# Output projection of an attention block: the two column halves of a token tile multiplied in one run of 48 products, the weights split in that order

## The chip, the cores and the metric

The kernel runs on one core of a Trainium2 chip. The metric is the device time of one execution in microseconds (us), the median of several runs. The engines are PE (TensorE: matmul products and transposes; PEld are its weight loads), ACT (ScalarE), DVE (VectorE), POOL (GpSimd) and SP (SyncE, which only issues DMAs here).

## The reference

One layer of a hybrid encoder block on x of 2048 tokens by 1024 columns, in float32:

```python
h = rms_norm(x, norm_mix_pre[l])
proj = h @ w_in[l]
...
mixed = jnp.concatenate([out_a, out_b], axis=-1) @ w_out[l]
x = x + rms_norm(mixed, norm_mix_post[l])
h = rms_norm(x, norm_ffn_pre[l])
f = (jax.nn.silu(h @ w_gate[l]) * (h @ w_up[l])) @ w_down[l]
x = x + rms_norm(f, norm_ffn_post[l])
```

`out_a` (512 columns) comes from sliding-window attention, `out_b` (512 columns) from differential attention. The change touches the third line alone, the product with `w_out` (1024 by 1024), and what surrounds it.

## The kernel before

The program is four stages, one after the other, with a barrier of all engines between them (`m.end()`): `proj_phase` (norm, projection, sliding-window attention), `diff_attn`, `out_proj` and `ffn`. Every engine has its own written-out program and they meet on semaphores, so the order of the work on each engine is the order of the code.

`out_proj` (line 1357) goes over 16 tiles of 128 tokens. It multiplies in float32 precision by splitting each operand into a high part (`_hi`) and the rest (`_lo`); one product becomes three, hi x hi, hi x lo, lo x hi (line 1662). For a tile k the steps are:

- SP loads the sliding-window part already transposed (`swa_in`) and the differential part by rows (`mix_in`), lines 1427 and 1428.
- PE transposes `mix_in` (`turn_m`, four transposes, line 1648). ACT makes `mt_hi` of both parts (`hi_m`, lines 1537 and 1539), POOL and DVE make `mt_lo` (`split_swa`, line 1485; `lo_m`, line 1592).
- PE multiplies: `multiply(n, k, i)` does column half n, 8 contraction chunks c by 3 products of 512 columns = 24 products into one PSUM bank. The stationary operand is the tile (`mt_hi` or `mt_lo`, chunk c), the moving one the weights.
- ACT sums the squares of y (`square_y`, line 1548), POOL makes the factor of the norm (`y_rstd_of`), DVE applies it (`norm_y`, line 1602), POOL adds x (`add_x`, line 1506).
- ACT sums the squares of the new x (`square_x`, line 1556), POOL makes the second factor (`x_rstd_of`, lines 160 and 162), DVE applies it and writes `h_row` (`norm_x`, line 1610).
- PE transposes `h_row` (`turn_h`, eight transposes, line 1674), ACT and DVE split the result (`hi_h`, `lo_h`, lines 1564 and 1617), SP stores it for the feed-forward stage.

The engines are staggered by one tile. In its pass k PE does `multiply(0, k)`, `turn_m(k+1)`, `multiply(1, k)`, `turn_h(k-1)`. In the same pass the others do, in this order:

```python
# ACT, lines 1575 to 1582
square_y(k - 1, i)
hi_m(k + 1, i)
square_x(k - 1, i)
hi_h(k - 1, i)
# DVE, lines 1630 to 1637
norm_y(k - 1, i)
lo_m(k + 1, i)
norm_x(k - 1, i)
lo_h(k - 1, i)
```

`hi_m(k+1)` waits in its middle, at line 1538, for `m_turned`, which `turn_m(k+1)` raises. y uses PSUM banks 0 to 3, so each tile has two of its own and the next tile the other two; the transposes use banks 4 to 6 in turn.

The weights come in 16 pieces of 128 by 512 (line 1373). Eight buffers hold them raw, ACT makes `w_hi` (line 1573), DVE `w_lo` (line 1627), each piece in turn. PE in tile 0 waits for each piece (line 1661).

Of the kernel before, what the change touches and what calls it, by code (L numbers as in the profile page):

```python
# [33 lines left out]
KC = D // P  # L34
# [21 lines left out]
def steady(count, k, i):  # L56

    return count(k) if i is None else (count(k + 2) - count(k)) * i + (4 * count(k) - 3 * count(k + 2))


def tiles(eng, first=0, end=TILES):


    for k in range(first, 6):
        yield k, None
    with eng.Fori(3, TILES // 2 - 1) as i:
        yield 6, i
        yield 7, i
    for k in range(TILES - 2, end):
        yield k, None  # L70
# [1286 lines left out]
def out_proj(nc, x, swa_t, mixed, w_out, subln, g_post, g_ffn, x_mid, h_s, h_hl):  # L1357
# [10 lines left out]
    y_banks, t_banks = Banks([0, 1, 2, 3], y_order), Banks([4, 5, 6], t_order)  # L1368
    SC = QA // P
    HW = D // 2  # L1370

    RAW = 8
    pieces = [(c, slice(n * HW, (n + 1) * HW)) for n in range(2) for c in range(KC)]

    with ExitStack() as ctx:
        m = Memory(nc, ctx, "op")
        ps = m.psum()
# [25 lines left out]
        w_hi_done, w_lo_done = m.sem("w_hi_done"), m.sem("w_lo_done")  # L1403
# [3 lines left out]
        m_turned, swa_hi, swa_lo, m_hi, m_lo = (m.sem(n) for n in ("m_turned", "swa_hi", "swa_lo", "m_hi", "m_lo"))  # L1407
        multiplied, y_squared, y_normed, pool_step, y_rstd_ready = (
            m.sem(n) for n in ("multiplied", "y_squared", "y_normed", "pool_step", "y_rstd_ready"))
# [6 lines left out]
        read_out = {"y": (y_normed, lambda t, n: 2 * t + n + 1), "m": (m_lo, lambda t: t + 1),  # L1416
                    "h": (h_lo, lambda t, n: 2 * t + n + 1)}

        with nc.Block() as block:
# [222 lines left out]
            @block.tensor  # L1642
            def _(pe):
                def turn_m(k, i):
                    pe.wait_ge(in_loaded[k % 2], steady(lambda t: 32 * (t // 2 + 1), k, i))
                    t_banks.free(pe, read_out, k, i, "m")
                    for j in range(DW // P):
                        last = pe.transpose(ps[:, t_banks.bank("m", k), j * P:(j + 1) * P],
                                            mix_in[:, k % 2, j * P:(j + 1) * P], ident[:, :])
                    last.then_inc(m_turned, 1)  # L1650

                def multiply(n, k, i):
                    q = k % 2
                    if n == 0:
                        pe.wait_ge(swa_lo, steady(lambda t: t + 1, k, i))
                    y_banks.free(pe, read_out, k, i, "y", n)
                    for c in range(KC):
                        if n == 0 and c == SC:
                            pe.wait_ge(m_lo, steady(lambda t: t + 1, k, i))
                        if k == 0:  # L1660
                            pe.wait_ge(w_lo_done, n * KC + c + 1)
                        for j, (lhs, rhs) in enumerate(((mt_hi, w_hi), (mt_hi, w_lo), (mt_lo, w_hi))):
                            last = pe.matmul(ps[:, y_banks.bank("y", k, n), :], lhs[:, q, c, :],
                                             rhs[:, c, n * HW:(n + 1) * HW],
                                             start=(c == 0 and j == 0), stop=(c == KC - 1 and j == 2))
                    last.then_inc(multiplied, 1)

                def turn_h(k, i):
                    pe.wait_ge(h_ready, steady(lambda t: t + 1, k, i))
                    for n in range(2):  # L1670
                        t_banks.free(pe, read_out, k, i, "h", n)
                        for j in range(4):
                            at = (4 * n + j) * P
                            last = pe.transpose(ps[:, t_banks.bank("h", k, n), j * P:(j + 1) * P], h_row[:, at:at + P],
                                                ident[:, :])
                        last.then_inc(h_turned, 1)

                pe.wait_ge(consts_made, 2)
                turn_m(0, None)
                for k, i in tiles(pe):  # L1680
                    multiply(0, k, i)
                    if k + 1 < TILES:
                        turn_m(k + 1, i)
                    multiply(1, k, i)
                    if k >= 1:
                        turn_h(k - 1, i)
                turn_h(TILES - 1, None)
# [316 lines left out]
def hybrid_block(nc, x, w_in, sinks, lambda_q1, lambda_k1, lambda_q2, lambda_k2, subln, w_out, g_mix_pre, g_mix_post,  # L2004
                 g_ffn_pre, g_ffn_post, w_gate, w_up, w_down, rope, out):

    def scratch(name, shape):
        return nc.dram_tensor(name, shape, F32, kind="Internal").ap()

    swa_t = scratch("swa_t", (P, QA // P, S))  # L2010
    q_s = scratch("q_s", (TILES, P, DH, 2, P))
    k_s = scratch("k_s", (P, DH, 2, S))
    v_s = scratch("v_s", (P, DH, TILES, VD))
    mixed = scratch("mixed", (S, DW))
    x_mid = scratch("x_mid", (S, D))
    h_s = scratch("h_s", (P, KC, 2, S))
    proj_phase(nc, x, w_in, g_mix_pre, sinks, rope, swa_t, q_s, k_s, v_s)
    diff_attn(nc, q_s, k_s, v_s, [lambda_q1, lambda_k1, lambda_q2, lambda_k2], mixed)
    with nc.sbuf_tensor("h_hl", [P, KC, 2, TB], F32R) as h_hl:
        out_proj(nc, x, swa_t, mixed, w_out, subln, g_mix_post, g_ffn_pre, x_mid, h_s, h_hl)  # L2020
        ffn(nc, h_s, h_hl, x_mid, w_gate, w_up, w_down, g_ffn_post, out)
# [40 lines left out]
```

## Time and profile before

| what | us |
|---|---|
| three runs: lowest, median, highest | 2763.47, 2764.42, 2766.68 |
| span of the profiled execution, first to last instruction | 2758.1 |
| PE busy in the span | 2567.2 (93%) |
| weight loads (PEld) busy | 2129.6 (77%) |
| DVE, ACT, POOL busy | 1265.5, 1082.0, 680.5 |

The profiled execution has only its span: the median of the runs lies 6.3 us above it, which is what surrounds the first and the last instruction and how one execution differs from another. `out_proj` takes from about 1057 us to 1283 us of the span. PE is busy almost all of the time, but that is an average over stages, and a stage has to be read by itself. "Granted clock" or PEclk is the clock that PE was given, as a share of 2.4 GHz: 1.0 is 2.4 GHz, 0.5 is 1.2 GHz. A timeline row gives the start, the length, the engine, the line, the operation with what it writes <- reads, and in brackets how long the engine sat idle before it and what ended that. Neighbouring rows of one kind are merged (x4).

### The profile page before, as it was taken

What the parts mean: (1) busy time and instruction counts of PE and PEld (TensorE: products, weight loads), DVE (VectorE), ACT (ScalarE), POOL (GpSimd) and SP (SyncE); (2) the same over time, 40 slices, a digit from 0 to 9 for tenths busy, and PEclk for the clock granted to TensorE, in tenths of its full rate; (3) what the DMA queues carried; (4) which work ended last, traced back from release to release, by engine and by line L of the source; (5) the groups of instructions that cost most, each with busy time, mean ns of one, the idle gap of its engine ahead of it and who ended that gap; (6) DMA issues with size and microseconds to landing.
All of it is one profiled execution on the core that took longest, in us unless ns stands there. A gap on an engine that the chain in (4) does not pass through costs nothing.

```text
span 2758.1 us, 38624 instructions
## 1 busy us (share of the span) xinstructions
PE 2567.2 (93%) x12588; PEld 2129.6 (77%) x12588; DVE 1265.5 (46%) x2315; ACT 1082.0 (39%) x2326; POOL 680.5 (25%) x827
## 2 busy tenths in 40 slices
PE   7999989996887887996999999999999999999997
PEld 5888867875776776885888888888888888888886
DVE  5667775556887884333222224222242222332223
ACT  5555563334666664332444223332222222233221
POOL 1323222223756654341111003110021110111101
PEclk9999989998999998998999999999999999999999
DMA  5111123334323214766333425334253343433332
GB/s 168 41 52 52 52 69 120 129 115 137 95 65 88 81 38 162 234 215 219 94 96 99 155 82 170 96 99 157 72 178 96 99 155 96 136 115 99 98 93 84
DMA packets 190193, 310.52 MB, mean 113 GB/s; under 512 B 15600, under 2 KB 119024, under 8 KB 190064
## 3 DMA queue, kind: packets, MB, share of 16 engines
q1 hardware_dynamic: 186608, 296.42, 34.3%
q0 software_dynamic: 3456, 12.58, 1.4%
q8 instruction: 56, 0.92, 0.1%
q14 instruction: 73, 0.60, 0.1%
HBM read 246.03 MB, written 62.91 MB: 112 GB/s over the span
## 4 chain that ended last, share of the span: by engine, by line
PE 52%; DVE 0%; issue 0%; DMA 0%; ACT 0%; POOL 0%; ACTq 0%; DVEq 0%; POOLq 0%
PE ff_psum L1963 35%; PE ff_psum L1993 17%; DVE ff_y L1917 0%; DMA ff_w_raw<-in_w_gate_dram 0%; DVE ff_y L1949 0%; DVE ff_y L1909 0%; ACT ff_junk L1861 0%; DVE ff_w_lo L1895 0%; ACT ff_w_hi L1888 0%; POOL ff_rstd L162 0%; ACTq L1741 0%; POOL ff_rstd L1819 0%; POOL ff_rstd L160 0%; ACTq L1844 0%; ACTq L1751 0%
## 5 line engine op out<-in xcount | busy, mean ns | idle before, releaser
L1963 PE MATMUL ff_psum<-h_hl,ff_w_hi 128*128 128x512 f32 x2816 | 869.4, 390 | 18.6 <-DVE ff_w_lo L1895 14.0
L1895 DVE TENSOR_TENSOR ff_w_lo<-ff_w_raw,ff_w_hi 128x1024 fp32r<-128x1024 f32 x264 | 328.5, 1246 | 986.0 <-ACT ff_w_hi L1845 974.4
L1963 PEld LDWEIGHTS ff_psum<-h_hl,ff_w_hi 128*128 128x128 f32 x2816 | 529.5, 188 | 130.1 <-DVE ff_w_lo L1895 14.4
L1845 ACT ACTIVATE ff_w_hi<-ff_w_raw 128x1024 fp32r<-128x1024 f32 x263 | 278.1, 1060 | 843.0 <-PE ff_psum L1963 500.0
L1963 PE MATMUL ff_psum<-h_hl,ff_w_lo 128*128 128x512 f32 x1408 | 548.7, 390 | 0.0
L1963 PEld LDWEIGHTS ff_psum<-h_hl,ff_w_lo 128*128 128x128 f32 x1408 | 265.0, 188 | 55.4
L1810 POOL TENSOR_TENSOR ff_g_lo<-ff_gated,ff_g_hi 128x512 f32 x88 | 113.4, 1290 | 759.5 <-ACT ff_g_hi L1852 759.2
L1993 PE MATMUL ff_psum<-ff_w_hi,ff_g_hi 128*128 128x512 f32 x704 | 273.9, 389 | 0.0
L1993 PE MATMUL ff_psum<-ff_w_lo,ff_g_hi 128*128 128x512 f32 x704 | 273.9, 389 | 0.0
L1993 PE MATMUL ff_psum<-ff_w_hi,ff_g_lo 128*128 128x512 f32 x704 | 273.9, 389 | 0.0
L1218 ACT ACTIVATE da_probs<-da_psum,da_bias 128x512 f32<-128x512 f32 (+3 forms) x320 | 196.1, 622 | 73.0 <-DVE da_bias L1270 60.8
L1264 DVE TENSOR_REDUCE da_tops<-da_psum 128x1 f32<-128x512 f32 (+3 forms) x288 | 173.8, 620 | 26.9 <-PE da_psum L1325 22.5
L1348 PE MATMUL da_psum<-da_values,da_at 128*128 (+1 forms) x1088 | 150.1, 281 | 19.1 <-ACT da_at L1226 11.0
L1348 PEld LDWEIGHTS da_psum<-da_values,da_at 128*128 128x128 f32 x1088 | 139.2, 194 | 34.6 <-issue 19.5
L1325 PE MATMUL da_psum<-da_keys,da_q_hl 128*128 (+3 forms) x320 | 139.4, 438 | 28.4 <-DMA da_keys<-k_s 16.8
L1993 PEld LDWEIGHTS ff_psum<-ff_w_lo,ff_g_hi 128*128 128x128 f32 x704 | 132.1, 188 | 27.6
L1993 PEld LDWEIGHTS ff_psum<-ff_w_hi,ff_g_lo 128*128 128x128 f32 x704 | 132.1, 188 | 27.4
L1993 PEld LDWEIGHTS ff_psum<-ff_w_hi,ff_g_hi 128*128 128x128 f32 x704 | 132.1, 188 | 27.3
L1325 PE MATMUL da_psum<-da_keys,da_q_lh 128*128 (+3 forms) x320 | 119.8, 377 | 0.0
L1184 POOL TENSOR_TENSOR da_probs<-da_probs 128x512 f32<-128x512 f32 (+2 forms) x96 | 116.7, 1216 | 8.0
L1852 ACT ACTIVATE ff_g_hi<-ff_gated 128x512 f32 (+1 forms) x88 | 55.6, 632 | 150.4 <-issue 150.4
L1819 POOL TENSOR_TENSOR ff_rstd<-ff_ss 128x4 f32<-128x4 f32 x4 | 0.8, 202 | 461.1 <-ACT ff_junk L1861 461.1
(192 smaller groups left out, 4215.4 us busy)
## 6 DMA issues: line engine op xcount, KB each, us to landing
ff_w_raw<-in_w_gate_dram SPq DMA_DIRECT2D x88, 512.0 KB, 3.6
ff_w_raw<-in_w_up_dram SPq DMA_DIRECT2D x88, 512.0 KB, 3.6
ff_w_raw<-in_w_down_dram SPq DMA_DIRECT2D x88, 512.0 KB, 3.6
pp_x<-in_x_dram SPq DMA_DIRECT2D x32, 512.0 KB, 4.7
h_s<-op_ht SPq DMA_DIRECT2D x16, 1024.0 KB, 6.2
h_hl<-h_s SPq DMA_DIRECT2D x3, 4096.0 KB, 14.4
pp_w_raw<-in_w_in_dram SPq DMA_DIRECT2D x32, 256.0 KB, 4.6
k_s<-pp_dk_hl SPq DMA_DIRECT2D x16, 512.0 KB, 4.0
```

What stands on the lines that cost most here:

```text
L1184: pool.tensor_tensor(probs[:, q, 0, cols], probs[:, q, 1, cols], probs[:, q, 0, cols], ALU.add)\
L1218: act.activation(probs[:, q, m, 4 * P * c:4 * P * c + w], ps[:, b, 0:w], ACT.Exp, bias=bias[:, r, m:m + 1], accum_out=sums[:, r, m, c:c + ...
L1264: top = dve.tensor_reduce(tops[:, r, m, c:c + 1], ps[:, b, 0:w], AX.X, ALU.max)
L1325: last = pe.matmul(ps[:, b, 0:w], stack[:, s % Q_SLOTS, m, :], keys[:, bass.ds(h, 1), m, 4 * P * c:4 * P * c + w].squeeze(1), start=(j == ...
L1348: last = pe.matmul(ps[:, O_BANK, 0:VD], at[:, n % A_SLOTS, j, :], values[:, bass.ds(h, 1), 4 * c + j, :].squeeze(1), start=(c == 0 and j = ...
L1810: pool.tensor_tensor(g_lo[:, bass.ds(f, 1), :].squeeze(1), gated[:, q, :], g_hi[:, bass.ds(f, 1), :].squeeze(1).bitcast(F32), ALU.subtract ...
L1819: pool.tensor_tensor(rstd[:, :], ss[:, 0, :], ss[:, 1, :], ALU.add).then_inc(pool_step, 1)
L1845: act.activation(w_hi[:, slot, :], w_raw[:, slot, :], ACT.Copy).then_inc(w_hi_done, 1)
L1852: act.activation(g_hi[:, bass.ds(f, 1), :].squeeze(1), gated[:, q, :], ACT.Copy).then_inc(g_hi_done, 1)
L1895: dve.tensor_tensor(w_lo[:, slot, :], w_raw[:, slot, :], w_hi[:, slot, :].bitcast(F32), ALU.subtract)\
L1963: last = pe.matmul(ps[:, u, :], w[:, u, at], h_hl[:, c, a, :], start=(c == 0 and n == 0), stop=(c == KC - 1 and n == 2))
L1993: last = pe.matmul(ps[:, bank, :], g[:, f, j * P:(j + 1) * P], w[:, u % R, rhs], start=(f == 0 and i == 0), stop=(f == FC - 1 and i == 2))
```

## The change

`multiply` takes both halves of a tile: for each chunk c and each of the three products it multiplies half 0 and then half 1 with the same stationary operand, 48 products in a row. Since there is only one run, `turn_m(k + 1)` stands behind all 48 instead of between the halves. The pieces of the weights are listed by chunk, then by half, and tile 0 waits for two pieces per chunk. Both banks have to be free, and `swa_lo` is waited for, before the first product; `m_lo` is waited for at chunk 4, which is now product 25 of 48. Nothing of ACT, DVE, POOL or SP is edited but the order of the 16 pieces.

```diff
@@ -1370,7 +1370,7 @@
     HW = D // 2
 
     RAW = 8
-    pieces = [(c, slice(n * HW, (n + 1) * HW)) for n in range(2) for c in range(KC)]
+    pieces = [(c, slice(n * HW, (n + 1) * HW)) for c in range(KC) for n in range(2)]
 
     with ExitStack() as ctx:
         m = Memory(nc, ctx, "op")
@@ -1649,21 +1649,23 @@
                                             mix_in[:, k % 2, j * P:(j + 1) * P], ident[:, :])
                     last.then_inc(m_turned, 1)
 
-                def multiply(n, k, i):
+                def multiply(k, i):
                     q = k % 2
-                    if n == 0:
-                        pe.wait_ge(swa_lo, steady(lambda t: t + 1, k, i))
-                    y_banks.free(pe, read_out, k, i, "y", n)
+                    pe.wait_ge(swa_lo, steady(lambda t: t + 1, k, i))
+                    for n in range(2):
+                        y_banks.free(pe, read_out, k, i, "y", n)
                     for c in range(KC):
-                        if n == 0 and c == SC:
+                        if c == SC:
                             pe.wait_ge(m_lo, steady(lambda t: t + 1, k, i))
                         if k == 0:
-                            pe.wait_ge(w_lo_done, n * KC + c + 1)
+                            pe.wait_ge(w_lo_done, 2 * c + 2)
                         for j, (lhs, rhs) in enumerate(((mt_hi, w_hi), (mt_hi, w_lo), (mt_lo, w_hi))):
-                            last = pe.matmul(ps[:, y_banks.bank("y", k, n), :], lhs[:, q, c, :],
-                                             rhs[:, c, n * HW:(n + 1) * HW],
-                                             start=(c == 0 and j == 0), stop=(c == KC - 1 and j == 2))
-                    last.then_inc(multiplied, 1)
+                            for n in range(2):
+                                last = pe.matmul(ps[:, y_banks.bank("y", k, n), :], lhs[:, q, c, :],
+                                                 rhs[:, c, n * HW:(n + 1) * HW],
+                                                 start=(c == 0 and j == 0), stop=(c == KC - 1 and j == 2))
+                                if c == KC - 1 and j == 2:
+                                    last.then_inc(multiplied, 1)
 
                 def turn_h(k, i):
                     pe.wait_ge(h_ready, steady(lambda t: t + 1, k, i))
@@ -1678,10 +1680,9 @@
                 pe.wait_ge(consts_made, 2)
                 turn_m(0, None)
                 for k, i in tiles(pe):
-                    multiply(0, k, i)
+                    multiply(k, i)
                     if k + 1 < TILES:
                         turn_m(k + 1, i)
-                    multiply(1, k, i)
                     if k >= 1:
                         turn_h(k - 1, i)
                 turn_h(TILES - 1, None)
```

PE in a pass before, from the last three products of half 0 to the first of the next tile (`op_mt` is the tile, `op_w` the weights, `op_mix_in` the rows that `turn_m` turns, `op_h_row` those of `turn_h`):

```order
L1663 MATMUL op_psum<-op_w_hi,op_mt_hi 128x512
L1663 MATMUL op_psum<-op_w_lo,op_mt_hi 128x512
L1663 MATMUL op_psum<-op_w_hi,op_mt_lo 128x512
L1648 MATMUL op_psum<-op_ident,op_mix_in 128x128 x4
L1663 MATMUL op_psum<-op_w_hi,op_mt_hi 128x512
...
L1663 MATMUL op_psum<-op_w_hi,op_mt_lo 128x512
L1674 MATMUL op_psum<-op_ident,op_h_row 128x128 x8
L1663 MATMUL op_psum<-op_w_hi,op_mt_hi 128x512
```

24 products stand between the two sets of transposes. PE at the same place now:

```order
L1664 MATMUL op_psum<-op_w_hi,op_mt_hi 128x512 x2
L1664 MATMUL op_psum<-op_w_lo,op_mt_hi 128x512 x2
L1664 MATMUL op_psum<-op_w_hi,op_mt_lo 128x512 x2
L1648 MATMUL op_psum<-op_ident,op_mix_in 128x128 x4
L1676 MATMUL op_psum<-op_ident,op_h_row 128x128 x8
L1664 MATMUL op_psum<-op_w_hi,op_mt_hi 128x512 x2
```

No product stands between them any more; they follow each other in this way in the passes k = 1 to 14. ACT in one pass, before and now alike (`op_y_junk` is `square_y`, `op_mt_hi` is `hi_m`, `op_x_junk` is `square_x`, `op_ht` is `hi_h`):

```order
L1548 ACTIVATE op_y_junk,op_y_ss<-op_psum 128x512 x2
L1537 ACTIVATE op_mt_hi<-op_swa_in 128x512
L1539 ACTIVATE op_mt_hi<-op_psum 128x512
L1556 ACTIVATE op_x_junk,op_x_ss<-op_x_new 128x1024
L1564 ACTIVATE op_ht<-op_psum 128x4x128 x2
```

On ACT nothing moved: the operation that needs the turned `op_mix_in` (L1539) stands ahead of the one that leads to `op_h_row` (L1556).

## Rows read from the trace of the kernel before

**Rows 1.** Busy time in a stretch of out_proj: length, then each engine, PEclk, DMA share, GB/s

```profile
core 0: us, PE busy (x) PEld busy (x) DVE busy (x) ACT busy (x) POOL busy (x), PEclk, DMA share, GB/s
...
1200.00:1260.00 60.00, 60.00 (x290) 49.08 (x289) 21.98 (x28) 22.05 (x49) 25.70 (x35) 1.00 0.61 198
```

**Rows 2.** Timeline, out_proj, one tile: start us, length us, engine, line, operation

```profile
1099.55 0.60 PE L1648 MATMUL op_psum<-op_ident,op_mix_in 128*128 128x128 f32 x4
...
1100.18 0.60 ACT L1539 ACTIVATE op_mt_hi<-op_psum 128x512 fp32r<-128x512 f32 x1 [3.72 <-PE op_psum L1648]
...
1101.21 1.06 ACT L1556 ACTIVATE op_x_junk<-op_x_new 128x1024 bf16<-128x1024 f32 x1 [0.43 <-POOL op_x_new L1506]
...
1103.38 1.29 DVE L1610 SCALAR_TENSOR_TENSOR op_h_row<-op_x_new,op_x_rstd,op_ffn_row 128x1024 f32<-128x1024 f32 x1 [1.88 <-POOL op_x_rstd L162]
...
1105.58 1.04 PE L1674 MATMUL op_psum<-op_ident,op_h_row 128*128 128x128 f32 x8
...
1112.06 0.60 PE L1648 MATMUL op_psum<-op_ident,op_mix_in 128*128 128x128 f32 x4
```

**Rows 3.** Timeline of PE, out_proj: the 24 products behind op_mix_in: first, second, last

```profile
1099.90 0.48 PE L1663 MATMUL op_psum<-op_w_hi,op_mt_hi 128*128 128x512 f32 x1
1100.22 0.39 PE L1663 MATMUL op_psum<-op_w_lo,op_mt_hi 128*128 128x512 f32 x1
...
1105.35 0.40 PE L1663 MATMUL op_psum<-op_w_hi,op_mt_lo 128*128 128x512 f32 x1
```

**Rows 4.** Page, costliest groups: products and weight loads of one stationary operand used twice

```profile
L1963 PE MATMUL ff_psum<-h_hl,ff_w_hi 128*128 128x512 f32 x2816 | 869.4, 390 | 18.6 <-DVE ff_w_lo L1895 14.0
...
L1963 PEld LDWEIGHTS ff_psum<-h_hl,ff_w_hi 128*128 128x128 f32 x2816 | 529.5, 188 | 130.1 <-DVE ff_w_lo L1895 14.4
```

**Rows 5.** Timeline of PE, feed-forward stage, up part (L1963)

```profile
1499.75 0.62 PE L1963 MATMUL ff_psum<-h_hl,ff_w_hi 128*128 128x512 f32 x2
```

**Rows 6.** Timeline of PE, feed-forward stage, down part (L1993): 12 products in a row

```profile
1599.71 0.39 PE L1993 MATMUL ff_psum<-ff_w_hi,ff_g_hi 128*128 128x512 f32 x1
...
1602.20 0.39 PE L1993 MATMUL ff_psum<-ff_w_hi,ff_g_lo 128*128 128x512 f32 x1
```

**Rows 7.** Timeline, end of out_proj: PE waits for h_row

```profile
1278.21 1.28 DVE L1610 SCALAR_TENSOR_TENSOR op_h_row<-op_x_new,op_x_rstd,op_ffn_row 128x1024 f32<-128x1024 f32 x1 [4.69 <-POOL op_x_rstd L162]
...
1279.55 1.97 PE L1674 MATMUL op_psum<-op_ident,op_h_row 128*128 128x128 f32 x8 [10.57 <-DVE op_h_row L1610]
```

**Rows 8.** Timeline of PE: idle times of earlier stages, with their releasers

```profile
370.76 0.66 PE L844 MATMUL pp_psum<-pp_ident,pp_probs 128*128 128x128 f32 x2 [4.18 <-DVE pp_o_sum L715]
...
691.87 0.33 PE L1336 MATMUL da_psum<-da_ident,da_probs 128*128 128x128 f32 x1 [2.38 <-POOL da_probs L1184]
...
837.68 0.58 PE L1348 MATMUL da_psum<-da_values,da_at 128*128 x1 [4.24 <-DVE da_at L1297]
...
943.00 0.72 PE L1348 MATMUL da_psum<-da_values,da_at 128*128 x2 [3.17 <-DVE da_at L1297]
```

**Rows 9.** Stretches right behind those idle times (columns as in rows 1)

```profile
370.76:376.28 5.52, 5.52 (x19) 4.77 (x20) 3.48 (x9) 3.89 (x8) 1.20 (x3) 0.50 0.29 92
...
837.68:840.49 2.81, 2.81 (x11) 2.51 (x12) 2.21 (x11) 0.40 (x2) 1.23 (x2) 0.50 0.00 0
...
943.00:946.31 3.31, 3.31 (x14) 3.01 (x15) 2.64 (x12) 0.56 (x4) 1.64 (x3) 0.52 0.04 9
...
691.87:695.30 3.43, 3.43 (x26) 3.18 (x26) 3.42 (x6) 2.58 (x9) 3.17 (x4) 1.00 0.00 0
```

**Rows 10.** Timeline, start of out_proj: products at the low clock, last weights

```profile
1067.15 0.76 PE L1663 MATMUL op_psum<-op_w_hi,op_mt_hi 128*128 128x512 f32 x1 [4.54 <-DVE op_w_lo L1627]
...
1067.71 0.63 PE L1663 MATMUL op_psum<-op_w_lo,op_mt_hi 128*128 128x512 f32 x1
...
1068.14 0.63 PE L1663 MATMUL op_psum<-op_w_hi,op_mt_lo 128*128 128x512 f32 x1
...
1077.13 2.78 DVE L1627 SCALAR_TENSOR_TENSOR op_w_lo<-op_w_raw,op_sub_col,op_w_hi 128x512 fp32r<-128x512 f32 x4
```

## The prediction

> **What bounds the kernel now.** I read the granted clock and the busy times first, then the stretches of the stage that the change touches, then its timeline. In `out_proj` PE is busy for the whole of each steady stretch at the full clock, while DVE, ACT and POOL are each busy for less than half of it [rows 1]. So in this stage any time in which PE newly waits is added to the kernel, and work saved on another engine is worth nothing.
>
> The timeline of one tile shows what this cover rests on [rows 2]. PE begins the transposes of tile k+1's `op_mix_in` at 1099.55, goes on with 24 products, and at 1105.58 begins the transposes of tile k-1's `op_h_row`. Between these two times the others work through a chain that begins with PE's own transposes: ACT L1539 starts at 1100.18, ACT L1556 at 1101.21, then POOL's two small steps, DVE L1610 from 1103.38 for 1.29 us. `op_h_row` is ready at 1104.67, 0.91 us before PE wants it. The next tile's transposes begin at 1112.06, so a tile costs 12.51 us.
>
> **The change, part by part.**
>
> *The products.* 48 a tile before and after, none removed and none added, and each half keeps its own 24. Behind `op_mix_in`, from the start of the second of 24 products to that of the last is 5.13 us for 22 steps, 0.233 us each [rows 3]. What could change is that the second product of a pair has the same stationary operand. The feed-forward stage shows such pairs: there each product has its own weight load, 2816 for 2816 [rows 4], and two of them together take 0.62 us where one takes 0.39, so the second starts 0.23 us after the first [rows 5]. The kernel before also uses `mt_hi[c]` for two products in turn at that even pace. I take 0. For the lower bound, the twelve down products step at 2.49 / 11 = 0.226 us [rows 6]: 768 products by 0.007 us would save 5.3 us. For the upper bound, the new order changes PSUM bank at each product. The down part changes bank after every six with nothing visible in its even steps; a change of bank costs 0.01 us there at most, the last digit of the rows, so at most 768 x 0.01 = 7.7 us.
>
> The Trainium skill, "TensorE: Matmul & The Clock Gate", section "Step-by-step: what each phase is for", says that the weight load is its own instruction because a loaded operand can serve many products. The trace shows no product without its load, so it has no case of this. The same page's Part 1 gives 215.7 ns from start to start of full-clock products of 512 columns; by that figure the run would gain 768 x 17.5 ns, an estimated 13.4 us.
>
> *The transposes of `op_mix_in` move behind product 48.* They are the same four; what moves with them is the start of the chain. ACT does L1539 (`hi_m`) before L1556 (`square_x`), so tile k-1's `square_x` cannot start until tile k+1's `op_mix_in` is turned, and `turn_h(k-1)` now stands right behind those four transposes. Counting from their start, T: ACT L1539 starts at T + 0.63 and takes 0.60; L1556 follows at about T + 1.23, since `add_x` has by then ended long ago (before, L1556 waited 0.43 us for it; now it has the time of 24 products more). From the start of L1556 to that of DVE L1610 is 1103.38 - 1101.21 = 2.17 us, L1610 takes 1.29 [rows 2], and PE starts 0.06 us after its end, as at the end of the stage [rows 7]. That is T + 4.75. Without a wait PE would go on at T + 0.35, as the first product behind the transposes does (1099.90) [rows 2, 3]. The new wait is 4.40 us of PE a tile. DVE's L1592 (`lo_m`) lies beside it and ends before L1610 can start. The wait occurs where both sets of transposes stand together: k = 1 to 14, 14 times, **61.6 us**. If ACT's two operations overlap somewhat it is 4.1 us (57.4 in all); if nothing of the 0.35 counts, 4.75 (66.5).
>
> Nothing else becomes late. Behind the wait stand `turn_h` and then tile k+1; its `mt_hi` and `mt_lo` are all made within the wait, so `m_lo` at product 25 costs nothing. ACT's `hi_h(k-1)` and `square_y(k)` lie behind `turn_h` as before, and the chain from there to `add_x` fits under the 48 products, 11.2 us. SP's loads for tile k+2 and its stores follow the same semaphores and have a whole tile. In the last pass there is no `turn_m`, so `turn_h(14)` has no new wait, and the last tile's idle time of 10.57 us [rows 7] stays: in both orders ACT takes both squares of tile 15 after `hi_h(14)`.
>
> *The clock.* PE did nothing for 4.18, 4.24 and 3.17 us in three places of the earlier stages [rows 8], and right behind each the granted clock was 0.50 to 0.52, which is the level of 1.2 GHz, for 5.52, 2.81 and 3.31 us of work, a mean of 3.88. After an idle time of 2.38 us it was 1.00 [rows 9]. The new waits are like the first three. At the low level a product takes 1068.14 - 1067.71 = 0.43 us instead of 0.233 [rows 10], so 0.455 of the time is lost. 3.88 x 0.455 = 1.76 us a wait, 14 times **24.7 us**. The bounds are the shortest and the longest stretch: 1.28 and 2.51 us, 17.9 and 35.1 in all.
>
> The same page, section "HAM oscillation — how this bites in real kernels", tells of a kernel whose PE waits in each pass and starts each pass at the low clock, and prices this at half of the low time. By that the term would be 14 x 3.88 x 0.5, an estimated 27.2 us. The rows' 0.455 is what I use.
>
> *The weights by chunk.* The first product now waits for two pieces, one more than at 1067.15; a piece is 2.78 / 4 = 0.70 us of DVE [rows 10]. These 0.70 us fall at the low clock, so some 1.6 products are put off, 1.6 x 0.233 = 0.4 us. At the far end the last piece is ready at 1077.13 + 2.78 = 1079.91 [rows 10] in both orders; three products stood behind it and now six do, at most 3 x 0.233 = 0.7 us more. I take **0.4 us**, between 0 and twice a piece, 1.4.
>
> *Sum.* 61.6 + 24.7 + 0.4 = 86.7 us, on a span of 2758.1: 2844.8. The 6.3 us by which the median lies above the profiled span are not touched, so 2764.4 + 86.7 = **2851 us**.
>
> **The rivals.**
>
> *The wait comes, the clock holds.* For it: the 2.38 us row. Against it: all three rows of over 3 us. 2764.4 + 61.6 + 0.4 = 2826 us.
>
> *The clock does not come back within a tile.* Then all 48 products run at 0.43 us, 9.4 us lost a tile: 2764.4 + 62 + 14 x 9.4 = 2958 us. Against it: behind every idle time of the rows the work brought the clock back in at most 5.52 us, and a tile has 11 us or more of dense products.
>
> *The reuse pays, and the kernel is not slower.* The mechanism is the second product of each pair going without the cost of a load, its place is the 384 second products. It has to give back 86.7 us, 0.226 us for each: they would have to be nearly free. The rows of pairs in the feed-forward stage show the second one at the full 0.23 us. If all it gave were the 0.007 us a product seen between stages, the time would be 2846. By the page's 215.7 ns it would be an estimated 2838. Should the four transposes not hold up `op_h_row` after all, so that this gain stood alone, the time would be 2764.4 + 0.4 - 5.3 = 2760 us; the order of ACT speaks against that.
>
> **How the numbers follow.** Forecast, wait and clock together: 0.89. Wait without the clock: 0.05. Clock stays down: 0.02. A small gain of pace beside the waits is inside the forecast. Not slower, by the last rival: 0.03, of which faster 0.02 and same 0.01; the remaining 0.01 is some other slower case. A measurement of this kernel tells about 0.2%, 5.5 us, from no change, so faster means under 2759 and slower over 2770: 0.02, 0.01, 0.97. The lower end is 2764.4 + 57.4 + 17.9 - 5.3 = 2834. The upper ends together are 2764.4 + 66.5 + 35.1 + 1.4 + 7.7 = 2875; all four at once is less likely than one of them, and I stop at 2870.
>
> **What would show each step.** In a timeline of a steady tile: four transposes, then an idle time of PE of about 4.1 us ended by DVE's `op_h_row` (L1610), then eight transposes; 14 such waits, 57 to 60 us, in the table of waits. ACT L1556 right behind L1539. PEclk near 0.5 just behind each wait and 1.0 before the end of the tile, a tile of 18 to 19 us instead of 12.5. Products at 0.233 us where the clock is full; 768 weight loads still. The stage ends some 87 us later, the others unchanged. I am wrong if `op_h_row` is ready when PE arrives, if the waits number other than 14, if the clock stays at 1.0, or if products at the full clock step at something other than 0.23 us.

## The result and the profile after

| | us |
|---|---|
| after, median of 4 runs (lowest, highest) | 2849.07 (2846.85, 2851.14) |
| before, median of 4 runs beside it | 2763.94 |
| ratio, 95% interval | 1.0313 (1.0301 to 1.0326) |
| span of the profiled execution, before and after | 2758.1, 2847.8 |

The change makes the kernel 85 us slower, 3.1%. Of all executions behind the figures of this document one, of e1 below, was slow (3298.40 us at a granted clock of 0.74) and is left out of its ratio. The first lines of the page after:

```profile
span 2847.8 us, 38628 instructions
...
PE 2599.4 (91%) x12588; PEld 2154.9 (76%) x12588; DVE 1266.2 (44%) x2315; ACT 1081.7 (38%) x2326; POOL 682.6 (24%) x827
```

PE is busy for 32 us more than before for the same products, and the span is 89.7 us longer. Neither says where; the stretches do. Up to 1057 us PE's busy time is 922.2 us before and 923.1 after, in the feed-forward stage 1440.1 and 1440.2. In `out_proj` it is 204.9 and 236.1.

The timeline of one tile after, all engines, at the place of [rows 2] (in the changed file the transposes of `op_h_row` are line 1676, the products line 1664; ACT, DVE and POOL keep their lines here):

```profile
1169.50 0.60 PE L1648 MATMUL op_psum<-op_ident,op_mix_in 128*128 128x128 f32 x4
1170.13 0.60 ACT L1539 ACTIVATE op_mt_hi<-op_psum 128x512 fp32r<-128x512 f32 x1 [10.04 <-PE op_psum L1648]
1170.63 1.05 ACT L1556 ACTIVATE op_x_junk<-op_x_new 128x1024 bf16<-128x1024 f32 x1
1170.76 0.69 DVE L1592 TENSOR_TENSOR op_mt_lo<-op_psum,op_mt_hi 128x512 fp32r<-128x512 f32 x1 [8.48 <-ACT op_mt_hi L1539]
...
1171.91 0.19 POOL L160 TENSOR_SCALAR op_x_rstd<-op_x_ss 128x1 f32<-128x1 f32 x1 [5.83 <-issue]
...
1172.77 1.28 DVE L1610 SCALAR_TENSOR_TENSOR op_h_row<-op_x_new,op_x_rstd,op_ffn_row 128x1024 f32<-128x1024 f32 x1 [1.32 <-POOL op_x_rstd L162]
...
1174.11 1.97 PE L1676 MATMUL op_psum<-op_ident,op_h_row 128*128 128x128 f32 x8 [4.02 <-DVE op_h_row L1610]
```

The transposes of `op_mix_in` start at 1169.50. ACT takes them at +0.63 and begins `square_x` (L1556) at +1.13, POOL's first step comes at +2.41, DVE's `op_h_row` at +3.27, and PE goes on at +4.61, idle for 4.02 us by the bracket. In [rows 2] the same operations stand between the same two points, with 24 products of PE beside them.

The table of waits in the stage (engine and line <- what it waited for: us in all, times, longest):

```profile
ACT op_mt_hi L1539 <- PE op_psum L1648: 149.6, 16, 11.1
...
PE op_psum L1676 <- DVE op_h_row L1610: 67.2, 15, 10.6
```

15 waits for `op_h_row`: the one of 10.6 us at the end of the stage, that was there before [rows 7], and 14 new ones that make up 56.6 us. ACT's wait for the turned `op_mix_in` went from 49.3 to 149.6 us, which costs nothing by itself: it is the other side of the same move, since ACT now stands at L1539 for the whole run of products, and `square_x` behind it.

Stretches after, in the columns of [rows 1]: products before a wait, the first and the second part of the wait, the work right behind it, the rest of the tile, and the work behind the next wait.

```profile
1159.00:1169.40 10.40, 10.40 (x46) 8.37 (x45) 1.56 (x3) 1.10 (x3) 4.57 (x5) 0.99 0.79 252
1170.11:1172.77 2.66, 0.00 (x0) 0.00 (x0) 0.69 (x1) 1.63 (x3) 0.74 (x2) 1.00 0.00 0
1172.79:1174.11 1.32, 0.00 (x0) 0.00 (x0) 1.27 (x1) 0.00 (x0) 0.00 (x0) 0.50 0.00 0
1174.11:1179.61 5.50, 5.50 (x17) 4.73 (x18) 1.64 (x3) 2.87 (x7) 0.94 (x3) 0.50 0.13 43
1179.62:1187.50 7.88, 7.88 (x35) 6.34 (x35) 1.14 (x2) 0.00 (x0) 3.64 (x2) 1.00 0.97 316
1193.49:1196.67 3.18, 3.18 (x12) 2.89 (x13) 1.24 (x2) 1.77 (x5) 0.00 (x0) 0.50 0.02 5
```

The granted clock is still 1.00 when the wait begins and falls to 0.50 before it ends; the work behind it then runs at 0.50, once for 5.50 us and once for 3.18. It fell in all 14 waits, 2.6 to 4.0 us after PE went idle. Read up to the rise of the clock, the low stretches of work alternate between 5.4 to 5.7 and 3.2 to 3.4 us, 4.36 us in the mean and 61.0 in all, against the 3.88 that the prediction took from [rows 9].

PE behind one of the waits, the turned tiles and then three pairs at the full clock:

```profile
1193.49 1.97 PE L1676 MATMUL op_psum<-op_ident,op_h_row 128*128 128x128 f32 x8 [4.12 <-DVE op_h_row L1610]
...
1197.77 0.63 PE L1664 MATMUL op_psum<-op_w_lo,op_mt_hi 128*128 128x512 f32 x2
1198.23 0.63 PE L1664 MATMUL op_psum<-op_w_hi,op_mt_lo 128*128 128x512 f32 x2
1198.70 0.63 PE L1664 MATMUL op_psum<-op_w_hi,op_mt_hi 128*128 128x512 f32 x2
```

Pairs start 0.46 to 0.47 us apart, 0.233 us a product, as in [rows 3]; the second product of a pair adds 0.23 us to the 0.39 or 0.40 of a single one. And the weight loads have not become fewer (the groups of the stage, PEld; one of three like it):

```profile
L1664 PEld LDWEIGHTS op_psum<-op_w_lo,op_mt_hi 128*128 128x128 f32 x256 | 54.5, 213 | 14.0
```

256 loads for 256 products. The stationary operand is used twice in a row and loaded twice.

### The profile page after: what moved, and what is told of

Its sections match the earlier page's. It is cut to its first block, busy times and chain, and to the rows that moved or that the text cites. A ratio compares the mean times of both kernels' runs of the same rounds, so it can differ in the third digit from the quotient of the medians.

```text
span 2847.8 us, 38628 instructions
## 1 busy us (share of the span) xinstructions
PE 2599.4 (91%) x12588; PEld 2154.9 (76%) x12588; DVE 1266.2 (44%) x2315; ACT 1081.7 (38%) x2326; POOL 682.6 (24%) x827
## 4 chain that ended last, share of the span: by engine, by line
PE 51%; DVE 0%; issue 0%; DMA 0%; ACT 0%; POOL 0%; ACTq 0%; DVEq 0%; POOLq 0%
PE ff_psum L1964 34%; PE ff_psum L1994 17%; DMA ff_w_raw<-in_w_gate_dram 0%; DVE ff_y L1918 0%; DVE ff_y L1950 0%; DVE ff_y L1910 0%; ACT ff_junk L1862 0%; DVE ff_w_lo L1896 0%; ACT ff_w_hi L1889 0%; POOL ff_rstd L162 0%; ACTq L1742 0%; POOL ff_rstd L1820 0%; POOL ff_rstd L160 0%; ACTq L1845 0%; ACTq L1752 0%
## 5 line engine op out<-in xcount | busy, mean ns | idle before, releaser
L1218 ACT ACTIVATE da_probs<-da_psum,da_bias 128x512 f32<-128x512 f32 (+3 forms) x320 | 196.1, 622 | 72.8 <-DVE da_bias L1270 60.8
L1325 PE MATMUL da_psum<-da_keys,da_q_hl 128*128 (+3 forms) x320 | 139.5, 438 | 28.1 <-DMA da_keys<-k_s 16.5
L1994 PEld LDWEIGHTS ff_psum<-ff_w_hi,ff_g_lo 128*128 128x128 f32 x704 | 132.2, 188 | 27.5
L801 PE MATMUL pp_psum<-pp_wv_hi,pp_xt_hi 128*128 128x512 f32 x256 | 107.5, 420 | 6.9 <-ACT pp_v_raw L513 6.9
```

Of the source, the lines that this page charges most:

```text
L801: last = pe.matmul(ps[:, b, 0:width], lhs[:, q, c, :], rhs[region][:, c, 0:width], start=(c == 0 and j == 0), stop=(c == KC - 1 and j == 2))
L1218: act.activation(probs[:, q, m, 4 * P * c:4 * P * c + w], ps[:, b, 0:w], ACT.Exp, bias=bias[:, r, m:m + 1], accum_out=sums[:, r, m, c:c + ...
L1325: last = pe.matmul(ps[:, b, 0:w], stack[:, s % Q_SLOTS, m, :], keys[:, bass.ds(h, 1), m, 4 * P * c:4 * P * c + w].squeeze(1), start=(j == ...
L1994: last = pe.matmul(ps[:, bank, :], g[:, f, j * P:(j + 1) * P], w[:, u % R, rhs], start=(f == 0 and i == 0), stop=(f == FC - 1 and i == 2))
```

## The experiments

Each kernel is set beside executions of the kernel before on the same chip. The earlier stages end up to 6 us apart from one execution to the next, so beside the medians I compare the stage alone: from PE's first transposes of `op_mix_in` to the start of the last ones of `op_h_row`, in the profiled execution. Tile 0, in which the weights arrive, takes 19.7 to 21.0 us in all of these executions but e6's; the last column leaves it out and starts at the first product of tile 1.

| kernel | median us | before beside it | ratio (95%) | stage us | first to last | from tile 1, us |
|---|---|---|---|---|---|---|
| before | | | | 218.0 | 1061.53 to 1279.55 | 198.1 |
| after | 2849.07 | 2763.94 | 1.0313 | 305.7 | 1063.13 to 1368.87 | 286.0 |
| e1, transposes back in the middle | 2762.75 | 2761.65 | 1.0004 (0.9995 to 1.0012) | 218.1 | 1066.72 to 1284.78 | 198.1 |
| e2, the move alone | 2848.82 | 2761.65 | 1.0321 (1.0306 to 1.0336) | 306.3 | 1061.01 to 1367.30 | 286.4 |
| e3, ACT and DVE reordered | 2761.79 | 2761.65 | 1.0006 (0.9996 to 1.0016) | 219.1 | 1062.60 to 1281.65 | 198.1 |
| e4, 16 filling products | 2824.48 | 2761.65 | 1.0229 (1.0214 to 1.0243) | 278.2 | 1066.69 to 1344.93 | 257.9 |
| e5, 8 filling products | 2828.13 | 2760.54 | 1.0244 (1.0228 to 1.0259) | 281.2 | 1061.97 to 1343.21 | 260.7 |
| e6, weights by half | 2857.78 | 2760.54 | 1.0350 (1.0335 to 1.0366) | 312.0 | 1065.46 to 1377.45 | 285.0 |
| e7, the end of before | 2760.64 | 2760.54 | 1.0001 (0.9992 to 1.0010) | 215.8 | 1066.37 to 1282.21 | 196.1 |

**e1: the transposes back between products 24 and 25.** Against the changed kernel:

```diff
                         if c == SC:
+                            if k + 1 < TILES:
+                                turn_m(k + 1, i)
                             pe.wait_ge(m_lo, steady(lambda t: t + 1, k, i))
...
                     multiply(k, i)
-                    if k + 1 < TILES:
-                        turn_m(k + 1, i)
```

> Keeps the 48 paired products and the weights by chunk, but puts the transposes of op_mix_in back in the middle of the tile, ahead of chunk 4, so that 24 products again stand between them and the transposes of op_h_row. If the new wait and the clock that falls in it are the whole loss, none of the 14 waits is left, PEclk is 1.0 in the stage, and the time is that of before plus the 0.4 us of the weights: 2764 to 2766 us. If the pairs or the change of bank at each product cost something beside the wait (up to 7.7 us by my bound) the time is up to 2772; if the reuse pays 5 us, 2760. If the loss had another cause than the place of the transposes, it stays near 2849.

Measured: 1.0004 of before, no new wait, and a stage of 218.1 us against 218.0. PE in one tile (op_mix_in is L1648, op_h_row L1678):

```profile
1110.88 1.04 PE L1678 MATMUL op_psum<-op_ident,op_h_row 128*128 128x128 f32 x8
...
1117.36 0.60 PE L1648 MATMUL op_psum<-op_ident,op_mix_in 128*128 128x128 f32 x4
...
1123.40 1.03 PE L1678 MATMUL op_psum<-op_ident,op_h_row 128*128 128x128 f32 x8
```

From one set of op_h_row to the next it is 12.52 us, the tile of before. So the pairs, the change of bank at each product and the weights by chunk, taken together, cost nothing that can be seen and give nothing. All of the loss is in the place of the four transposes.

**e2: the move alone.** Against the kernel before:

```diff
                     multiply(0, k, i)
+                    multiply(1, k, i)
                     if k + 1 < TILES:
                         turn_m(k + 1, i)
-                    multiply(1, k, i)
```

> The kernel before with one edit: the transposes of op_mix_in stand behind both halves. Products and weights as before, 24 and 24. By the theory of the wait this alone gives nearly all of the change: 14 waits of 4.0 to 4.1 us of idle PE, low clock behind each, 2849 us within 2. By the rival, that the run of 48 paired products matters for the clock or the pace, it differs from 2849 by more than 5 us.

Measured: 2848.82 us, stage 306.3 us, and in its table of waits the same row as after's:

```profile
PE op_psum L1674 <- DVE op_h_row L1610: 67.2, 15, 10.6
```

The one edit gives the whole change.

**e3: PE as changed, ACT and DVE in another order.** `hi_m` is cut before its wait for the turned rows; the second part is `hi_mix`. Against the changed kernel:

```diff
 # ACT
                         hi_m(k + 1, i)
                     if k >= 1:
                         square_x(k - 1, i)
+                    if k + 1 < TILES:
+                        hi_mix(k + 1, i)
+                    if k >= 1:
                         hi_h(k - 1, i)
 # DVE
+                    if k >= 1:
+                        norm_x(k - 1, i)
                     if k + 1 < TILES:
                         lo_m(k + 1, i)
                     if k >= 1:
-                        norm_x(k - 1, i)
                         lo_h(k - 1, i)
```

> The changed kernel on PE, but on ACT square_x(k-1) stands ahead of the step that waits for the turned op_mix_in (L1539), and on DVE norm_x(k-1) ahead of lo_m(k+1). Then op_h_row does not hang on the transposes. If the order on ACT and DVE makes the wait, the 14 waits go and the time is 2764 to 2766 us with PE's order of after unchanged; the chain for m_lo, 0.63 + 0.60 + 0.69 us, lies under 8 transposes and 24 products. If PE's wait came from the transposes themselves or from a PSUM bank, it stays at 2849.

Measured: 1.0006 of before, no new wait. Its timeline at one tile (in its file L1559 is `square_x`, L1617 `norm_x`, L1656 the transposes of op_mix_in, L1684 those of op_h_row, L1542 the former L1539):

```profile
1116.03 1.06 ACT L1559 ACTIVATE op_x_junk<-op_x_new 128x1024 bf16<-128x1024 f32 x1 [4.77 <-POOL op_x_new L1506]
...
1118.19 1.28 DVE L1617 SCALAR_TENSOR_TENSOR op_h_row<-op_x_new,op_x_rstd,op_ffn_row 128x1024 f32<-128x1024 f32 x1 [4.76 <-POOL op_x_rstd L162]
...
1119.88 0.60 PE L1656 MATMUL op_psum<-op_ident,op_mix_in 128*128 128x128 f32 x4
...
1120.32 1.04 PE L1684 MATMUL op_psum<-op_ident,op_h_row 128*128 128x128 f32 x8
...
1120.52 0.60 ACT L1542 ACTIVATE op_mt_hi<-op_psum 128x512 fp32r<-128x512 f32 x1 [3.34 <-PE op_psum L1656]
```

`op_h_row` is ready at 1119.47, before PE begins the transposes of `op_mix_in`, and the two sets stand together without a wait. So it is not the transposes on PE, nor their PSUM banks, that make the wait, but the order on ACT and DVE: `square_x(k-1)` stands behind the wait for the turned rows on ACT, and `norm_x(k-1)` behind `lo_m(k+1)` on DVE. e3 moves both at once, so it does not show what either move is worth alone. In the timeline after, DVE is done with `lo_m` (L1592) at 1171.45 and idle for 1.32 us before L1610, until POOL's factor is there, so what ends last is the chain through `square_x`. The stage is 1.1 us longer than before's, all of it in tile 0, where PE waited 0.46 us for a piece of the weights (0.26 us in the profile after, none in e1's); from tile 1 on both take 198.1 us.

**e4: the wait filled.** Against the changed kernel:

```diff
                         turn_m(k + 1, i)
+                        if k >= 1:
+                            for _ in range(16):
+                                pe.matmul(ps[:, 7, :], w_hi[:, 0, 0:P], w_hi[:, 0, 0:HW], start=True, stop=True)
                     if k >= 1:
                         turn_h(k - 1, i)
```

> The changed kernel with 16 products of constant weights into the unused PSUM bank 7 between the two sets of transposes in the passes 1 to 14; they add work without use, and the output is unchanged. 16 x 0.233 = 3.7 us, so they lie inside the wait of about 4.3 us and PE has some 0.4 us idle. The h row comes no earlier. If the second term is the clock, PEclk stays at 1.0 and the time is 2764.4 + 0.4 + 14 x 4.26 = 2824 us, 25 us faster than after although PE does 224 products more. If the low clock is not what the tiles lose, it stays at 2849; if the products delay something, it is over that.

Measured: 2824.48 us. PE at one tile, and the stretch of ten tiles, e4's and then after's:

```profile
1131.89 0.60 PE L1648 MATMUL op_psum<-op_ident,op_mix_in 128*128 128x128 f32 x4
1132.24 3.90 PE L1688 MATMUL op_psum<-op_w_hi 128*128 128x512 f32 x16
1136.51 1.10 PE L1676 MATMUL op_psum<-op_ident,op_h_row 128*128 128x128 f32 x8 [0.36 <-DVE op_h_row L1610]
```

```profile
1110.00:1270.00 160.00, 156.45 (x726) 125.55 (x725) 43.27 (x56) 41.17 (x93) 50.92 (x67) 1.00 0.53 172
```

```profile
1110.00:1270.00 160.00, 123.54 (x507) 100.40 (x507) 40.14 (x50) 37.81 (x84) 43.25 (x58) 0.87 0.46 149
```

`op_h_row` still comes 4.62 us behind the first transposes, but PE is idle for 0.36 us only and the clock is 1.00 in the whole stretch, where after it was 0.87. This kernel does 224 products more than the changed one and is 24 us faster (e2, which has the same waits as the changed kernel, took 2848.82 us on the same chip). It separates the two terms. From tile 1 on, e4 - e3 is the wait, 257.9 - 198.1 = 59.8 us, and after - e4 is the clock, 286.0 - 257.9 = 28.1 us. With tile 0 in it, the whole stage gives 59.1 and 27.5.

**e5: the wait half filled.** As e4 with `range(8)`.

> As the kernel with 16 filling products, but with 8, so that PE is idle for 4.02 - 8 x 0.233 = about 2.2 us at each of the 14 places; the output is unchanged. The tile still waits for the same op_h_row, so the wait term stays 59 to 60 us. If the low clock comes only behind longer idle times, as it did not come behind the 2.38 us of rows 9, the time is 2824 us as with 16. If 2.2 us are enough to lose it every time, PE's low stretches return and the time is near 2849. Between the two: it is lost in some tiles and held in others, some 1.8 us for each that loses it.

Measured: 2828.13 us. In the profiled execution PE is idle for 2.16 to 2.28 us at the 14 places. The clock held at 12 of them and fell at two; a tile where it held, the work behind the wait where it fell, and the rest of that tile:

```profile
1165.40:1182.00 16.60, 14.56 (x68) 11.66 (x68) 4.49 (x6) 4.39 (x10) 5.31 (x7) 1.00 0.76 253
1182.24:1185.37 3.13, 3.13 (x12) 2.84 (x13) 1.18 (x2) 1.72 (x5) 0.00 (x0) 0.50 0.34 136
1185.40:1200.43 15.03, 12.87 (x58) 10.10 (x57) 3.55 (x5) 2.75 (x7) 5.32 (x7) 1.00 0.55 174
```

The two tiles that lost it took 18.19 and 18.28 us instead of 16.75 to 16.85, 1.5 us each, which is the 3.0 us between the stages of e5 and e4. The profiled execution is the fastest of the four (2824.56 to 2829.53 us), so the others may have lost the clock more often; no trace shows them. So the outcome is the mixed one of the expectation: at an idle time of about this length the clock falls at some places and not at others.

The kernel before shows the same. PE is idle for 2.38 or 2.39 us at four places of its differential-attention stage, each ended by POOL's `da_probs`; [rows 8, 9] have only the first. The 3 us behind each:

```profile
691.87:694.87 3.00, 3.00 (x22) 2.79 (x23) 3.00 (x5) 2.58 (x9) 2.83 (x3) 1.00 0.00 0
790.65:793.65 3.00, 3.00 (x22) 2.78 (x23) 3.00 (x5) 2.65 (x9) 2.83 (x3) 1.00 0.02 5
895.68:898.68 3.00, 3.00 (x11) 2.65 (x12) 2.42 (x4) 2.77 (x9) 2.83 (x3) 0.50 0.00 0
1000.38:1003.38 3.00, 3.00 (x13) 2.56 (x14) 2.88 (x4) 2.66 (x9) 2.83 (x3) 0.63 0.00 0
```

The clock held at two of them, was 0.50 from the start at the third and fell within a microsecond at the fourth.

**e6: the weights by half with the paired products.** Against the changed kernel:

```diff
-    pieces = [(c, slice(n * HW, (n + 1) * HW)) for c in range(KC) for n in range(2)]
+    pieces = [(c, slice(n * HW, (n + 1) * HW)) for n in range(2) for c in range(KC)]
...
-                            pe.wait_ge(w_lo_done, 2 * c + 2)
+                            pe.wait_ge(w_lo_done, KC + c + 1)
```

> The changed kernel with the weights made in the old order, by half, and tile 0 waiting for piece 8 + c + 1 of them. Its first product needs piece 9, which ends at about 1074.33 + 0.68 = 1075.0 on the scale of before, instead of piece 2 at about 1067.8: 7.2 us later. Products then step faster than the pieces come. PE would begin at the low clock and lose up to 2.5 us there, against about 2 us in after, so tile 0 ends some 7 us later and the time is 2856 us (2853 to 2858). If the order of the weights did not matter it would be 2849.

Measured: 2857.78 us, stage 312.0 us, 6.3 more than after's, where I expected 7. PE's first transposes and first pair:

```profile
1065.46 1.08 PE L1648 MATMUL op_psum<-op_ident,op_mix_in 128*128 128x128 f32 x4 [10.06 <-DMA op_mix_in<-mixed]
1079.52 1.19 PE L1664 MATMUL op_psum<-op_w_hi,op_mt_hi 128*128 128x512 f32 x2 [12.98 <-DVE op_w_lo L1627]
```

12.98 us idle instead of the 4.11 of after. Part of it is made up: PE then waits for no further piece, and the clock rises 2.84 us after its first product instead of 5.45. In all tile 0 is 7.2 us longer, as expected, and from tile 1 on the kernel is 1.0 us shorter, because the clock fell late at the first wait and stayed low for 3.4 us. The ratios to before put the difference at some 10 us (1.0350 against 1.0313), with 6 us of noise either way. The order by chunk is thus needed with the pairs, and worth about 6 us there; with it the pairs are no faster than the kernel before (e1).

**e7: the end of the stage.** Against the kernel before:

```diff
 # ACT
                         square_x(k - 1, i)
+                        if k == TILES - 1:
+                            square_y(k, None)
                         hi_h(k - 1, i)
-                square_y(TILES - 1, None)
 # DVE
                         norm_x(k - 1, i)
+                        if k == TILES - 1:
+                            norm_y(k, None)
                         lo_h(k - 1, i)
-                norm_y(TILES - 1, None)
```

> The kernel before with one edit at its end: in the last pass ACT takes the squares of tile 15 ahead of hi_h(14) and DVE does norm_y(15) ahead of lo_h(14), since PE's last idle time of 10.57 us hangs on that chain. The first of POOL's steps for tile 15 could start at about 1269.1 instead of 1270.89 and the idle time be some 1.8 us shorter, 8.8 us. The time would be 1.8 us less, 0.07%, which a run can hardly tell from no change; the trace can. If another wait ends the chain, the idle time stays at 10.6 us.

Measured: the last wait is 8.59 us instead of 10.57, and the stage 2.2 us shorter, 2.0 of them from tile 1 on:

```profile
1272.79 0.60 ACT L1548 ACTIVATE op_y_junk<-op_psum 128x512 bf16<-128x512 f32 x1 [2.39 <-PE op_psum L1665]
...
1273.56 0.19 POOL L1494 TENSOR_TENSOR op_y_rstd<-op_y_ss 128x1 f32<-128x1 f32 x1 [2.77 <-ACT op_y_junk L1548]
...
1282.21 1.97 PE L1676 MATMUL op_psum<-op_ident,op_h_row 128*128 128x128 f32 x8 [8.59 <-DVE op_h_row L1611]
```

In the time of the whole it cannot be told from before: 1.0001, with an interval of 0.1% either way. It is the same mistake of order in small (an operation whose input is ready stands behind one whose input is late), and a gain that only the trace shows. No version that I ran is measurably faster than the kernel before.

## Why the prediction was right

The forecast was 2851 us; 2849.07 was measured. The mechanism came as forecast, its terms were off by 2 to 3 us each. Point by point:

- *The products at 0.* Right: 0.233 us each at the full clock, 768 loads, and by e1 the stage with pairs is 218.1 us against 218.0. Neither the 5.3 us that I allowed for as a gain nor the 7.7 us for the banks came. By the Trainium skill's 215.7 ns ("TensorE: Matmul & The Clock Gate", Part 1) there would have been an estimated 13.4 us to gain. The traces do not agree: the steady pace of this stage at the full clock was 0.233 us a product in every kernel here, with and without pairs.
- *The wait, 61.6 us.* The mechanism is shown: e2 makes it with the one edit, e3 takes it away with an edit on ACT and DVE alone. The size is 59.8 us by e4 and e3, 4.27 us a tile where the sum had 4.40. What was too large is mostly the step from ACT L1539 to L1556: I took the full 0.60 us of the first, but the second started 0.50 us after it. The text had named such an overlap for its lower bound, 4.1. The 14 waits have 56.6 us in the table of waits, just under the 57 to 60 named as the sign; the table counts from the end of the transposes, the sum from where the next product would have started.
- *The clock, 24.7 us.* It fell at each of the 14 waits, as the three rows over 3 us suggested, and cost 28.1 us, 2.01 a wait instead of 1.76. The mis-sized part is the low time. The stretches of [rows 9] end before the clock rises; it is still 0.50 up to here:

```profile
370.76:376.46 5.70, 5.70 (x20) 4.90 (x21) 3.66 (x9) 4.07 (x9) 1.20 (x3) 0.50 0.28 89
837.68:840.68 3.00, 3.00 (x12) 2.70 (x13) 2.37 (x12) 0.40 (x2) 1.42 (x2) 0.50 0.00 0
943.11:946.51 3.40, 3.40 (x15) 3.10 (x15) 2.53 (x12) 0.45 (x3) 1.77 (x3) 0.50 0.01 3
```

Their mean is 4.0 us, not 3.88, and the 14 new ones have 4.36. With the 61.0 us that these make up, the rows' 0.455 gives 27.8 us, close to the 28.1. By the rule of half the low time in the Trainium skill ("TensorE: Matmul & The Clock Gate", section "HAM oscillation — how this bites in real kernels") it would be an estimated 30.5 us, 2.4 too many. The rival in which the clock holds was set against the one row of 2.38 us; of the four such idle times in the trace two lost the clock (e5 above), so that row spoke for it less than it seemed.
- *The weights, 0.4 us.* Not measurable: from PE's first transposes to the first product of tile 1 it is 19.8 us after (1063.13 to 1082.91) and 19.9 before (1061.53 to 1081.43).
- *Nothing else late.* Right: `out_proj` is the only stage whose busy time changed, and the idle time at its end is 10.58 us as before.

- *The 6.3 us between span and median.* Taken as fixed, and it was not: after, the median lies 1.3 us above the profiled span. The time of an execution is 1.5 to 1.6 us above its own span in every run here, so the rest of the 6.3 was that the profiled execution of the kernel before was a short one.

Two terms were off in opposite directions, the wait by 1.8 us too much and the clock by 3.4 too little. The spans differ by 89.7 us where the sum had 86.7, 1.6 of it because the earlier stages happened to end later; the medians differ by 85.1. That the forecast came within 2 us of the median is therefore partly luck; the mechanism, shown by e2, e3 and e4, is not. The rival of the wait without the clock, 2826 us, is what e4 shows with 2824.48: its price was right, and only what PE does during the wait decides between it and the forecast. The rival of a gain from reuse has nothing for it in e1, nor in the pace within a pair.

## What to carry to other kernels

Before moving work on the bottleneck engine, follow what it releases: here four small transposes started a chain over ACT, POOL and DVE that was hidden only by the 24 products behind them, and the order of the code on ACT put tile k-1's norm behind tile k+1's transposes. Where the two must stand together, put the operation whose input is ready ahead of the one that waits on the other engines; here that took the whole loss back (e3, 1.0006 of before). And price a new wait on PE with the work at the low clock behind it: it added almost half again to the wait itself.

## What the runs showed of the hardware

- Using a stationary operand for two products in a row does not change the pace of this kernel, as each product still has its own weight load: 0.233 us with and without, in two banks by turns or in one.
- Useless products can pay: 16 of them in each wait took 24 us off the changed kernel by keeping the granted clock at 1.00. It still was 2.3% slower than the kernel before.
- With 2.2 us of idle time at the same place in each tile the clock fell at 2 of 14 places in the one execution profiled; with 2.39 us in the kernel before at 2 of 4; with 4.0 to 4.1 us at 14 of 14; with 0.3 to 0.5 us at none. Places that look alike in a timeline need not behave alike.
- The low stretches behind equal waits alternated between about 5.5 and 3.2 us, and the tiles with them between about 19.3 and 18.2 us. One such row would have mispriced the term by a quarter either way.
